# Sixteen expert rounds in place of seventeen, with a third tile of rows in one of them, and another schedule of a mixer's steps

## The reference

```python
for i in range(DEPTH):                        # DEPTH = 2
    mod = silu(c) @ ada_w[i] + ada_b[i]
    sh1, sc1, g1, sh2, sc2, g2 = split(mod, 6)
    h = modulate(x, norm_mix_g[i], sh1, sc1)
    m, S = retention_mixer(...) if i == 0 else gla_mixer(...)
    x = x + g1[:, None, :] * m
    h = modulate(x, norm_ffn_g[i], sh2, sc2)
    x = x + g2[:, None, :] * moe_ffn(h, ...)
return rmsnorm(x, final_norm_g), new_ret, new_gla

def moe_ffn(h, ...):                          # 64 experts, 8 per token
    scores = sigmoid(x @ w_router); biased = scores + router_bias
    # the 4 best of 8 groups, then the 8 best experts in them
    wsel = scores[chosen] / sum * 2.5
    # per expert e: its tokens' rows x_e
    routed[tokens] += w * ((silu(x_e @ w_gate[e]) * (x_e @ w_up[e])) @ w_down[e])
    return routed + (silu(x @ ws_gate) * (x @ ws_up)) @ ws_down
```

## Time and profile before

| | |
|---|---|
| median of 3 runs | 1741.76 us (1740.02 to 1741.95) |
| the profiled execution | 1741.48 us |
| its span in the profile | 1739.6 us |
| mean granted TensorE clock | 0.982 of full speed |
| PE busy | 1622.3 us, 93% of the span |
| weight loads (PEld) | 1091.0 us, 63% |
| DVE, ACT, POOL busy | 751.5 (43%), 382.1 (22%), 97.6 us (6%) |
| HBM read, written | 594.42 MB, 26.90 MB: 357 GB/s over the span |

### The profile page before, as it was taken

One profiled execution on the slowest core, in us unless ns is written; L12 is line 12 of the kernel. 1 busy time (PEld: TensorE's weight loads), 2 busy tenths in 40 slices (PEclk: granted clock), 3 DMA queues, 4 the chain that ended last, 5 costly groups with the idle time before them and its releaser, 6 DMA issues. The chain is left out here.

```text
span 1739.6 us, 29551 instructions
## 1 busy us (share of the span) xinstructions
PE 1622.3 (93%) x11480; PEld 1091.0 (63%) x11480; DVE 751.5 (43%) x1860; ACT 382.1 (22%) x804; POOL 97.6 (6%) x118
## 2 busy tenths in 40 slices
PE   7998899999999999999998899989999999999996
PEld 4776665777566555565665587766656566566563
DVE  2204435216644435435345235357553534534435
ACT  2012343112211112112112336231111211112112
POOL 0000110000000000000000001011000000000000
PEclk9999899999999999999999899999999999999998
DMA  9994599338999999999997784688999999999970
GB/s 368 384 369 169 204 395 403 115 141 331 421 419 420 421 419 417 420 420 413 420 419 307 248 263 139 244 328 331 421 420 420 421 420 420 418 418 416 418 323 26
DMA packets 154111, 603.96 MB, mean 347 GB/s; under 512 B 18253, under 2 KB 63473, under 8 KB 101690
## 3 DMA queue, kind: packets, MB, share of 16 engines
q1 hardware_dynamic: 137354, 559.89, 81.0%
q0 software_dynamic: 16064, 40.92, 6.2%
q10 hardware_dynamic: 624, 2.23, 0.3%
HBM read 594.42 MB, written 26.90 MB: 357 GB/s over the span
## 5 line engine op out<-in xcount | busy, mean ns | idle before, releaser
L2269 PE MATMUL ps<-ring,scratch 128*64 128x256 f32 x4352 | 485.3, 382 | 26.2 <-DMA ring<-in_moe_w_up 24.4
L2269 PEld LDWEIGHTS ps<-ring,scratch 128*64 128x64 f32 x4352 | 333.7, 138 | 164.8 <-issue 37.1
L2301 PE MATMUL ps<-ring,scratch 128*64 128x512 f32 x1088 | 243.6, 598 | 3.5 <-DVE scratch L2625 1.8
L2250 PE MATMUL ps<-scratch 128*128 128x264 bf16 x1632 | 196.6, 277 | 4.5 <-issue 4.1
L2595 DVE SCALAR_TENSOR_TENSOR scratch<-scratch,ps 128x256 f32<-128x256 f32 x68 | 32.7, 482 | 381.9 <-ACT scratch L2709 381.8
L734 PE MATMUL ps<-hT,ring 128*128 128x264 f32 x768 | 183.4, 396 | 1.3 <-ACT hT L371 1.3
L2250 PEld LDWEIGHTS ps<-scratch 128*128 128x128 bf16 x1632 | 141.9, 97 | 63.6 <-issue 19.7
L734 PEld LDWEIGHTS ps<-hT,ring 128*128 128x128 f32 x768 | 149.6, 196 | 30.3 <-issue 1.6
L2301 PEld LDWEIGHTS ps<-ring,scratch 128*64 128x64 f32 x1088 | 70.6, 136 | 148.8 <-issue 104.1
L2566 DVE TENSOR_TENSOR scratch<-scratch,ps 128x264 f32<-128x264 f32 x256 | 109.9, 429 | 57.8 <-PE ps L2250 57.8
L2709 ACT ACTIVATE scratch<-ps 128x256 f32<-128x256 f32 x68 | 26.2, 385 | 482.5 <-PE ps L2269 482.5
(11 more groups left out here) (345 smaller groups left out, 1320.8 us busy)
## 6 DMA issues: line engine op xcount, KB each, us to landing
ring<-in_moe_w_gate SPq DMA_DIRECT2D x136, 1024.0 KB, 18.6
ring<-in_moe_w_up SPq DMA_DIRECT2D x136, 1024.0 KB, 17.8
ring<-in_moe_w_down SPq DMA_DIRECT2D x136, 1024.0 KB
ring<-in_ada_w SPq DMA_DIRECT2D x48, 1024.0 KB, 12.8
ring<-in_ret_w_in SPq DMA_DIRECT2D x24, 1024.0 KB, 16.7
ring<-in_state_ret SPq DMA_DIRECT2D x16, 1024.0 KB, 15.2
out_ret_sample<-ring POOLq DMA_DIRECT2D x16, 1024.0 KB, 9.0
ring<-in_gla_w_in SPq DMA_DIRECT2D x12, 1024.0 KB, 11.9
```

The costliest lines, as they stand in the source:

```text
L2250: mm = nc.tensor.matmul(k.ps[:, c % 2, 0:T], row_parts[:, p, s, c * P:(c + 1) * P], slot_token[:, p, :], start=(p == 0 and s == 0), stop=( ...
L2269: mm = nc.tensor.matmul(k.ps[lo:lo + CAP, 2 + p, j * DE:(j + 1) * DE], xg[:, p, c, lo:lo + CAP], slot(k, n, DE)[:, c, :], start=(c == 0), ...
L2301: mm = nc.tensor.matmul(k.ps[lo:lo + CAP, 6 + half, :], hid_t[:, p, m, lo:lo + CAP], slot(k, n, D)[:, m, half * 512:(half + 1) * 512], sta ...
```

## The change

**Experts.** The 17th round is gone (LAST = 15). A new `list_order` on DVE writes the order in which the experts go through the rounds: experts 0 to 3 stay in round 0, the three fullest of the others take the first three places of round 7 (HEAVY), the rest fill up in order of their numbers. In round 7 the three fullest have a third tile of rows on the same weights: 64 more rows for the first, 32 more for each of the other two (`HEAVY_TILE`). It has its own gate, up and down products (L2336 and L2389 in the new file), a third fetch and gather in round 6, and a share in round 8's spread; the slots of its weights are freed only after it. Since the experts of a round are no longer neighbours, their numbers are read with `value_load`, four per round on SP (ahead of the loads) and four per round on DVE (in `next_slots`), and the slots and weights are made expert by expert. `find_blocks` and `block_weights` are gone; `count_blocks` and `find_experts` go to rounds 1 and 2 and serve the extra part alone, where experts have still more rows. Rounds 5 to 8 are written out; the others before and behind run in loops.

**Mixer.** The 32 units are given to the steps by `UNITS_FROM`: two each from t = 12 to 15, three each from 16 to 23. A unit's `spread_value` stands inside a projection; in DVE's order the state updates stand ahead of the rotation, and ACT's copy of the last sample values at the start of t = 12; the reads are at other steps.

Core of the diff:

```diff
+HEAVY = 7
+HEAVY_TILE = [(0, 0, 64), (1, 64, 32), (2, 96, 32)]
...
-SAMPLES_HEAD_AFTER = {9: 0, 10: 1, 11: 2, 12: 3}
-STATES_AT = {13: [0], 14: [1], 15: [2, 3], 16: [4], 17: [5, 6], 18: [7], 19: [8, 9], 20: [10], 21: [11, 12], 22: [13],
-             23: [14, 15]}
-READS_AT = {16: [0], 17: [1], 18: [2], 19: [3], 21: [4], 22: [5], 23: [6]}
+SAMPLES_HEAD_AT = {9: 0, 10: 1, 11: 2, 12: 3}
+UNITS_FROM = {12: 0, 13: 2, 14: 4, 15: 6, 16: 8, 17: 11, 18: 14, 19: 17, 20: 20, 21: 23, 22: 26, 23: 29, 24: 32}
+STATES_AT = {t: range((UNITS_FROM[t] + 1) // 2, (UNITS_FROM[t + 1] + 1) // 2) for t in range(12, 24)}
+READS_MID = {16: [0]}
+READS_AT = {16: [1], 18: [2], 19: [3], 20: [4], 22: [5], 23: [6]}
...
-                for u in us[:len(us) // 2]:
+                for u in us[0:1]:
                     spread_value(u)
                 project(t, 0, 2 * (t % 2), first.s_h if t == 0 else None)
-                for u in us[len(us) // 2:3]:
+                if t in SAMPLES_HEAD_AT:
+                    sample_values(SAMPLES_HEAD_AT[t])
+                for u in us[1:2]:
                     spread_value(u)
                 project(t, 1, 2 * (t % 2) + 1).then_inc(k.ring_free[loads[t] % RING], 1)
-                for u in us[3:]:
-                    spread_value(u)
...
+                    pause = (5, 3)[m]
+                    project(t, m, gate_bank(n), chunks=range(pause))
+                    spread_value(us[m + 1])
+                    mm = project(t, m, gate_bank(n), chunks=range(pause, DC))
+                    if m == 0:
+                        for b in READS_MID.get(t, []):
+                            read(b)
+                mm.then_inc(k.ring_free[loads[t] % RING], 1)
...
+                if t in SAMPLES_HEAD_AT:
+                    place_values(SAMPLES_HEAD_AT[t])
+                    split_values(SAMPLES_HEAD_AT[t])
+                for u in units_at(t):
+                    update(u)
                 if t < 4 or t >= 12:
                     rotate(t)
...
             load_until(k, sp, n_sh + 3 + RING)
+            sp.wait_ge(s_count, 1)
             with sp.Fori(1, ROUNDS) as r:
+                expert_of = [expert_at(sp, r * EPI + e) for e in range(EPI)]
                 for name, e in ROUND:
                     n = place(name, e)
-                    src = expert_weight(name, r * EPI + e)
+                    src = expert_weight(name, expert_of[e])
                     sp.wait_ge(k.ring_free[n % RING], r + n // RING)
                     sp.dma_start(slot(k, n, src.shape[2]), src).then_inc(k.ring_full[n % RING], 16)
-
-
-            sp.wait_ge(s_count, 1)
-            extra_of = [block_expert(sp, 1 + e) for e in range(EPI)]
-            for name, e in ROUND:
-                n = place(name, e) + ROUNDS * RING
-                src = expert_weight(name, extra_of[e])
-                sp.wait_ge(k.ring_free[n % RING], n // RING)
-                sp.dma_start(slot(k, n, src.shape[2]), src).then_inc(k.ring_full[n % RING], 16)
...
+            if heavy:
+                pe.wait_ge(s_hid, d + 1)
+                for j, name in enumerate(("moe_w_gate", "moe_w_up")):
+                    for c in range(DC):
+                        for e, lo, wide in HEAVY_TILE:
+                            n = place(name, e)
+                            mm = nc.tensor.matmul(k.ps[lo:lo + wide, 2, j * DE:(j + 1) * DE],
+                                                  xg_of(PAIRS)[:, c, lo:lo + wide], slot(k, n, DE)[:, c, :],
+                                                  start=(c == 0), stop=(c == DC - 1))
...
+                if heavy and p == 0:
+                    hidden_first(pe, PAIRS, 3, d)
+                    pe.wait_ge(s_rhi, 2 * d + 1)
+                    slots_first(pe)
+            if heavy:
+                pe.wait_ge(s_hidtc, d + 3)
+                for half in range(2):
+                    pe.wait_ge(s_rest, 2 * d + 2 * (PAIRS - 1) + half + 1)
+                    for m in range(FC):
+                        for e, lo, wide in HEAVY_TILE:
+                            n = place("moe_w_down", e)
+                            mm = nc.tensor.matmul(k.ps[lo:lo + wide, 6 + half, :], hid_t[:, PAIRS, m, lo:lo + wide],
+                                                  slot(k, n, D)[:, m, half * 512:(half + 1) * 512],
+                                                  start=(m == 0), stop=(m == FC - 1))
+                            if m == FC - 1 and half == 1:
+                                mm.then_inc(k.ring_free[n % RING], 1)
+                    if half == 0:
+                        mm.then_inc(s_dn, 1)
...
+        def slots_of(to, at_, of, e, wide):
+
+            return nc.vector.tensor_tensor(to, of[:, :, bass.ds(e, 1)].to_broadcast([P, TT, wide]),
+                                           slot_number[:, 0:wide].unsqueeze(1).to_broadcast([P, TT, wide]),
+                                           ALU.is_equal)
+
+        def weights_of(to, e):
+
+            return nc.vector.tensor_copy(to, w_parts[:, :, bass.ds(e, 1), :].rearrange("p t o s -> p t (o s)"))
...
+        def list_order(v):
+
+            link = lambda ins: k.dve.link(v, ins)
+            link(nc.vector.scalar_tensor_tensor(load_key, count, float(NE), iota[:, 0:NE], ALU.mult, ALU.add))
+            link(nc.vector.memset(load_key[:, 0:EPI], -1.0))
+            link(nc.vector.max(out=heaviest, in_=load_key))
...
+            h0 = HEAVY * EPI
+            nc.vector.tensor_copy(order[0:1, 0:h0], others[:, 0:h0])
+            nc.vector.tensor_copy(order[0:1, h0:h0 + 3], heavy_ids[0:1, 0:3])
+            nc.vector.tensor_copy(order[0:1, h0 + 3:NE], others[:, h0:NE - 3]).then_inc(s_count, 1)
+            v.wait_ge(s_count, 1)
...
+                of = [expert_at(v, r * EPI + e) for e in range(EPI)]
                 v.wait_ge(s_ht, r)
-                round_weights(w_parts[:, :, bass.ds(r * EPI, EPI), :])
-                one_hot(v, r)
...
+                for e in range(EPI):
+                    weights_of(eye_w[:, e // 2, :, P + 3 * (e % 2):P + 3 * (e % 2) + 3], of[e])
+                if tiles(r) > PAIRS:
+                    for e, lo, wide in HEAVY_TILE:
+                        weights_of(eye_w3[:, :, P + 3 * e:P + 3 * e + 3], of[e])
+                        slots_of(hot3[:, :, lo:lo + wide], lo, over, of[e], wide)
+                for e in range(EPI):
+                    ins = slots_of(hot[:, :, e, :], 0, left, of[e], CAP)
+                ins.then_inc(s_hot, 1)
...
+                if heavy:
+                    v.wait_ge(h_done, H_SLOTS)
+                    link(own_third())
+                    hidden(PAIRS, d)
+                elif more:
+                    next_slots(r + 2)
...
+                    if heavy and q == 1:
+                        next_slots(r + 2)
...
             v.sem_inc(s_add, DC)
+            list_order(v)
             next_slots(1)
             v.wait_ge(s_idx, 2)
             row_numbers(PAIRS, bank=0).then_inc(s_idxc, 1)
-            count_blocks(v)
             take(v, 0, 0, nc.vector.tensor_copy, g_even)
-            find_experts(v)
-            find_blocks(v)
-            round_(0, True, False, True, next_slots, (0,))
-            round_(1, False, False, True, next_slots, (1, 2))
-            round_(2, False, False, True, next_slots, (3,))
-            with v.Fori(3, ROUNDS - 2) as r:
-                round_(r, False, False, True, next_slots)
-            round_(ROUNDS - 2, False, False, True, extra_slots)
-            round_(ROUNDS - 1, False, False, True, None)
-            round_(LAST, False, True, False, None)
+            round_(0)
+            round_(1, beside=count_blocks)
+            round_(2, beside=find_experts)
+            with v.Fori(3, HEAVY - 2) as r:
+                round_(r)
+            for r in range(HEAVY - 2, HEAVY + 2):
+                round_(r)
+            with v.Fori(HEAVY + 2, LAST - 1) as r:
+                round_(r, late=1)
+            round_(LAST - 1)
+            round_(LAST)
```

More of the change, by code:

```diff
@@ L704, in units_at @@
     def units_at(t):
[L705 removed]
+        return range(UNITS_FROM[t], UNITS_FROM[t + 1]) if t in STATES_AT else []
     with nc.Block() as block:
@@ L2195, in _ @@
                 if r:
-                    pool.wait_ge(s_gat, 4 * r)
-                for p in range(PAIRS):
+                    pool.wait_ge(s_gat, 2 * done_tiles(r, 0))
+                for p in range(tiles(r)):
                     fetch_rows(pool, p, s_got, rows_at if r else first_rows_at)
@@ L2233, in spread_slots, with third_slots_first @@
             return mm
+        def third_slots_first(pe, r):
+            pe.wait_ge(s_htc, r + 1)
+            for t in range(TT):
+                n = P if t < 2 else NS
+                mm = nc.tensor.matmul(k.ps[:, 4, (t + 1) * EW3 - 9 - n:(t + 1) * EW3], hot3[:, t, :],
+                                      eye_w3[:, t, P - n:EW3], start=True, stop=True)
+            mm.then_inc(h_done, 1)
         def slots_first(pe):
@@ L2416, in rows_done, with take @@
```

(23 more changed lines are left out.)

404 lines of the change are left out of this document (224 added, 180 removed).

## The result

The changed kernel takes 1750.26 us (median of 5 runs, 1749.32 to 1752.73), the kernel before 1741.62 us in the same session (5 runs): ratio 1.0054, 95% interval 1.0040 to 1.0069. It is slower by 8.6 us, where 1754 was forecast, 12 us more than before.

The account below looks back on a forecast made before the run. PE was taken to bound a round at 30.3 us, the weight stream close behind at 31.7. From 1741.5, +31.6 for both layers' rounds and starts and -19.0 for the mixer gave 1754.1, so 1754; 8-in-10 range 1718 to 1783.

Parts of the forecast that it names:

- One period less: Expert rounds: the 17th round goes, saving one 30.3 us period and most of 15 us of waits per layer.
- next_slots: DVE in the rounds: register loads and slots delay the rest of pair 0 by 1.8 or 1.3 us, 20.4 per layer.
- The third tile: Mainly round 7: unequal column tiles do not run side by side, 1.1 us a triple; with surrounding work +34.6 us per layer.
- Rival A: Third tile's products: the three widths run side by side, 2 x 14.6 us less, 1725; chance 0.24.
- Start of a layer: Before round 1's list: PE stands 4.4 us for DVE's work, plus 1.3 of slow clock, +5.7 us per layer.
- The mixer: Retention mixer before the experts: the new schedule removes PE's waits and the slow clock behind them, -19 us.
- The rounds: Expert rounds of a layer: 504.7 us against 494.6, +10.1 per layer.
- B: Register loads in the rounds: each costs 0.55 us and waits for the datapath, 47 us more at most, 1790; chance 0.11.
- C: Mixer: the pauses make PE stand for the same ACT products elsewhere, -5 instead of -19, 1768; chance 0.08.
- D: Register loads in the rounds: they hide or cost half, and the stream limits; up to 46 less, 1708; chance 0.10.
- E: Extra part: experts overflow the third tile and leave blocks for extra pairs, 30 us and more, 1785 and up; chance 0.02.

Follow-up runs that it names:

- early loads: The changed kernel with DVE's four register loads per round moved ahead of the hidden values' products, where DVE waits for ACT: 1722.74 us.
- doubled loads: The changed kernel with each of DVE's register loads done twice in the same place: 1856.24 us.
- sorted order: The changed kernel with all 64-wide tiles of a third-tile product first, then all of the two 32-wide ones: 1741.90 us.
- equal widths: The changed kernel with the third tile's products all 32 columns wide, the first expert's 64 rows as two tiles: 1718.38 us.
- late list: The changed kernel with PE listing round 1's rows behind the first gather, not in the middle of the shared expert's product: 1737.12 us.
- the run of its own: The kernel before with the change's edits to the mixer and no other: 1723.97 us.

## Why the prediction was right, and where not

The forecast of 1754 went by a sum of five terms, and the sign hung on two of them.

- **One period less.** Right: 15 rounds in place of 16 lie between the first round's start and the last one's, and the waits for expert weights, 24.4 us, are gone. The argument that longer rounds leave the stream time held: in a loop DMA moves 412 GB/s and PE waits for none of it, and where early loads brought the rounds back to 30.4, with the same 24 MB fewer to load, 10.0 us of these waits came back.
- **next_slots.** The mechanism was right, the size a little too large. I took the rest of pair 0 to be 1.8 us late in loops and 1.3 in written-out rounds, and rounds of 32.1 and 31.6. (By its own terms the first is 598.57 - 596.86 = 1.7, a slip of 0.1 per round.) Measured: 1.4 late in the loop round shown, and rounds 1.4 and 1.0 longer than the forecast's 30.3, 31.74 and 31.34. A load takes 0.30 us, not the 0.32 I took, and with all around it 2.9 us for four; and the small copies overlap each other more, 0.59 for four in place of 0.68. What I wrote to look for, a wait of PE of 2 us or more per round, was wrong: it is 1.1, since the 0.67 of the earlier trace rows was idle time of the weight load alone: the matmuls' waits for that line were 1.8 us in all. Early loads showed that this is the loads' place, doubled loads that it is their number.
- **The third tile.** The products were right: 1.13 us a turn against 1.1, 18.1 against 17.6 for gate and up, a wait of 2.75 against 3.0 for the rests, and 8.0 against 7.7 for down at the full clock. The down products took 9.4 because the sum had the stop of 3.0 us but no clock behind it, 1.45 us per layer. Rival A, the widths side by side, is refuted by the traces of this run and of the sorted order; and equal widths show what it would have been worth, 31.9 us where I priced the rival at 29. The Trainium skill's rule ("TensorEngine Tiling (Array Packing)", "Key Properties") that a change of tiling mode drains TensorE agrees with these runs: the 64-wide and the 32-wide tiles did not overlap, and each change cost 0.13 us besides.
- **Start of a layer.** The stop of 4.4 us was 4.65 and 4.1 (8.7 in two), but what the clock costs behind it was taken too small: 1.3, by a row where 2.1 stood; measured 6.79 less 3.81, 3.0. The late list took back 7.6 and 7.1 us in the traces (6.6 per layer by the medians), against the 5.7 forecast.
- **The mixer.** -19 forecast, -17.1 in the trace and -17.7 in the run of its own. The waits for ACT and DVE went as a whole, but for 0.5 us. I took 5 us off the full 24 for the pace of DVE and ACT; the size came out, the reason did not. What was left were 5.7 us of waits for the projections' weights, which the term did not have: its room for the stream was a mean over 132 us, and they fall in the 70 us in which DMA moves 400 GB/s. That the stream's rate holds these weights back, and not the time at which their slots come free, is not shown by a run of its own.

The sum in the traces: mixer -17.1, starts +14.9 (7.8 and, by the late list, 7.1), rounds +13.4, the rest between and behind the layers' rounds -1.3: +9.9, against -19, +11.4, +20.2 and 0, +12.6. The rounds came out 6.8 us below their term; the starts came out 3.5 and the mixer 1.9 us above theirs. That these partly cancel, so that the total is nearer than its terms, is luck. Rivals B, C, D and E did not happen: the loads don't wait for the datapath (the first begins at 814.28, while the copy of gathered rows runs until 814.85) and take 0.30 us and not 0.55, the mixer's waits went, the loads don't hide where they stand, and PE runs no product of the extra part. The Trainium skill ("Runtime: NRT & Kernel Launch", "Instruction fetch mechanics") gives about 200 ns for a register load; the median of 120 here is 302 ns, and the measurement decides.

## What to carry to other kernels

Removing a whole round of an engine that is the bound is worth the round only as long as its work does not come back dearer elsewhere; here it came back in one round that took twice as long, because a 64-wide column tile and two 32-wide ones did not run side by side. A small serial thing, such as reading four numbers into registers, costs nothing on an engine that idles half the time, unless it stands between that engine's last and next service to the bound engine; look for the wait that it stands ahead of, and for the idle stretch (4.8 us here) in which it would be free. Price a stop of TensorE with its clock: 4.65 us of standing cost 3 us more behind it, 2.75 us cost 1.45 more. And a mean over a long stretch can hide that the weight stream is full in half of it.

## What the runs showed of the hardware

- A column tile of 64 and one of 32 columns don't run at the same time; four of 32 do, in the time of one (0.44 us for one turn of products with 256 float32 columns moving, 0.43 for the 64-wide alone). A change between the widths costs 0.13 us besides. Split in two, the 64-wide tile ran beside the others, and a turn took 0.44 us in place of 1.13.
- Four register loads on DVE take 2.9 us in a loop, 0.71 from one to the next, of which the load is 0.30. They run while the datapath still copies, but the copies and compares behind them in DVE's order wait for them (2.34 us of idle datapath ahead of 817.19).
- The granted clock was at its lower level (about 0.5) behind stops of 4.65 us (6.79 us for 3.81 of work), of 3.55 us (6.49 for 3.65) and of 2.75 us (9.43 for 7.98); after the 1.2 us stops of the changed kernel's rounds it stayed at 1.00. In the run with doubled loads two stops of 3.63 us were followed by 5.17 and by 3.73 us for the same product, so a stop's length alone does not tell what it costs.
